# Feed-forward layers of a two-block network as one single chunk and five adjacent pairs, with another order of products inside a pair

## The chip, the cores and the metric

One Trainium2 chip, one of its cores. The metric is the device time of one execution in microseconds (us). Everything is computed in float32 inputs split into two parts (a "hi" part rounded to fp32r and a "lo" remainder), and one matrix product is made of three passes: hi x hi, lo x hi, hi x lo.

## The reference, cut to what matters

256 tokens of 1024 features run through two layers (a convolution module or an attention module, then a gated feed-forward network, then a small gate) and a second block. The change touches the two feed-forward networks alone:

```python
D_MODEL, SEQ, DEPTH = 1024, 256, 2
D_FF = 2816
def swiglu(x, w_gate, w_up, w_down):
    return (jax.nn.silu(x @ w_gate) * (x @ w_up)) @ w_down
...
u = rms_norm(h, ffn_norm_g[i])
h = h + swiglu(u, ffn_w_gate[i], ffn_w_up[i], ffn_w_down[i])
```

## The kernel before, in words

The 2816 hidden features of a layer are cut into 11 chunks (0 to 10) of 256; a chunk's 512 weight columns hold 256 of the gate and 256 of the up projection. The tokens are two tiles (t 0 and 1) of 128, the 1024 input features two halves.

**Weights.** A piece is 128x2048 float32 (1 MB). SP loads pieces into a ring of four (`raw`, line 385); the load of a piece waits until the lo part of the one four earlier is made. For each operand ScalarE (ACT) makes `w_hi` (line 1297) and then VectorE (DVE) `w_lo` (line 1857), both into rings of three: the hi part of operand g waits until TensorE (PE) is through with operand g-3. Both engines take the operands in stream order, at the places where the program calls `ahead(g)`, which feeds up to g+2. Each engine's instructions run in the order written, so an operand that is late holds up everything behind it.

**A single chunk** (`single`, `token_chunk`) is 48 matmuls of 512 columns: 2 halves x 2 tiles x 4 x 3 passes. A **pair** of chunks (`pair`, `product`) does the work of 96 in seven products of 12: B11, T1, T2, B22, B21, T4, T3. B11, B21 and B22 are pieces as loaded. T1 to T4 are sums of pieces, kept in three slots of `arena`: slot 0 for T1, slot 1 for T2 and then T3, slot 2 for T4. GpSimd (POOL) makes them with DMAs: a plain load and an accumulating one for T1 (lines 1164, 1106) and T4 (1168, 1109), one accumulating DMA on top of T2 for T3 (1156). DVE makes T2 out of T1 and the raw B22 (`second_sum`, line 1994). POOL issues them in this order for each next pair: T1's load (once T1's lo part is made), T3's addition (once T2's lo part is made), T1's addition, T4's load (once T4's lo part is made), T4's addition.

The products of a pair go to three of the PSUM banks 0 to 2 (b1, b4, b2), which rotate from pair to pair. Quarters are put together by ACT copies (`c_11` L1400, `c_22` L1404, `c_12` L1409) and DVE sums (L2046, L2049, L2038). `gated` (ACT silu L1361, DVE L1979) turns a quarter into the hidden values of one chunk and token tile. The last quarter, out of T3's bank, is gated by `last_quarter`, which runs on both engines at the start of the next step.

**Down projection.** `hidden_job(i)` (L603) transposes a chunk's hidden values, `hidden_hi` and `hidden_lo` (L1353, L1972) split them, `down(i)` is 24 matmuls of line 441 into banks 4 to 7. The steps of a layer are single 0, single 1, pairs (2,3), (4,5), (6,7), (8,9), single 10, and the order within a pair is

```python
product p1 B11; hidden_job(turned[0])
product p5 T1; product p6 T2; hidden_job(turned[1])
product p3 B22; down(within[0])
product p2 B21; product p7 T4; down(within[1])
product p4 T3
```

In the first feed-forward layer POOL issues, behind the last third sum, one further DMA that the attention needs much later (`toep`, line 1177).

## Time and profile before

| | |
|---|---|
| time, median of 3 runs | 1003.75 us (1002.15 to 1005.62) |
| the profiled execution's own time | 1003.63 us |
| its span | 1001.6 us |
| granted TensorE clock | 0.999 of full speed |
| busy: PE, DVE, ACT, POOL | 988.1, 775.3, 609.2, 153.6 us |
| first feed-forward layer (109.67 to 288.07 us) | 178.40 us |
| second feed-forward layer (429.39 to 605.35 us) | 175.96 us |

The span is the time from the first to the last instruction; about 2 us of the execution lie around it. A line of a timeline gives start, duration, engine, line, operation, tiles out<-in, shapes, and in brackets how long the engine had been idle and who ended that. Durations of neighbours overlap: one 512-column matmul is shown with 0.39 us though they start 0.227 us apart. So a product's length is read from start to start.

### The profile page before, as it was taken

To read this page: it belongs to the slowest core of one execution; us is meant where nothing else is said; L and a number is where in the kernel's file an instruction comes from. 1 tells how busy PE (TensorE), PEld (TensorE's weight loads), DVE (VectorE), ACT (ScalarE), POOL (GpSimd) and SP (SyncE) were. 2 spreads that over 40 slices of the span, in tenths; PEclk is the share of its full clock that TensorE was granted. 3 is DMA by queue.
4 is the path that set the end of the run, shared out by engine and by line. 5 is a ranking of instruction groups with operands and counts; after the bars stand their busy time and mean duration, and the time that the engine had idled before them with its cause. 6 is when DMAs were issued, how large, how long until landed. Compare 5 with 4: busy or idle time off the path is not lost.

```text
span 1001.6 us, 13597 instructions
## 1 busy us (share of the span) xinstructions
PE 988.1 (99%) x5350; PEld 835.5 (83%) x5350; DVE 775.3 (77%) x909; ACT 609.2 (61%) x722; POOL 153.6 (15%) x150
## 2 busy tenths in 40 slices
PE   8999999999999999999999999999999999999997
PEld 8977888888778888788888888788888889999886
DVE  6996888879567666787988857876877788777874
ACT  6437567657376668666676646754857574444733
POOL 4992101101030320111111002100100010000000
PEclk9999999999999999999999999999999999999999
DMA  8862899999784632779999864577789898545631
GB/s 324 256 217 90 274 298 324 334 300 305 209 292 161 238 128 85 256 264 300 331 343 338 256 218 167 189 256 280 262 258 341 237 311 299 186 169 179 220 126 43
DMA packets 37726, 242.01 MB, mean 242 GB/s; under 512 B 4504, under 2 KB 7064, under 8 KB 9760
## 3 DMA queue, kind: packets, MB, share of 16 engines
q1 hardware_dynamic: 23904, 167.26, 43.8%
q0 software_dynamic: 10736, 70.71, 28.2%
q10 hardware_dynamic: 3024, 3.18, 1.3%
q8 instruction: 43, 0.70, 0.3%
q14 instruction: 19, 0.16, 0.0%
HBM read 237.91 MB, written 3.21 MB: 241 GB/s over the span
## 4 chain that ended last, share of the span: by engine, by line
PE 80%; DVE 8%; DMA 6%; issue 3%; ACT 1%; POOL 0%; SPq 0%; ACTq 0%; POOLq 0%; DVEq 0%
PE bank L441 45%; PE bank L564 18%; DVE bank L2160 4%; PE bank L427 4%; PE bank L429 4%; PE bank L428 4%; DMA raw<-in_ws 4%; DMA arena<-in_ws 3%; PE bank L478 2%; DVE w_lo L1857 2%; PE bank L603 1%; PE bank L847 0%; DMA u_scr<-arena 0%; PE bank L944 0%; PE bank L977 0%
## 5 line engine op out<-in xcount | busy, mean ns | idle before, releaser
L1857 DVE TENSOR_TENSOR w_lo<-raw,w_hi 128x2048 fp32r<-128x2048 f32 x145 | 332.8, 2303 | 84.0 <-ACT w_hi L1297 83.7
L1297 ACT ACTIVATE w_hi<-raw 128x2048 fp32r<-128x2048 f32 x156 | 298.2, 1912 | 107.9 <-PE bank L441 71.3
L1297 ACT ACTIVATE w_hi<-arena 128x2048 fp32r<-128x2048 f32 x48 | 92.4, 1924 | 57.2 <-PE bank L441 21.0
L441 PE MATMUL bank<-w_hi,x_hi 128*128 128x512 f32 x416 | 115.0, 398 | 0.2
L1857 DVE TENSOR_TENSOR w_lo<-arena,w_hi 128x2048 fp32r<-128x2048 f32 x48 | 109.2, 2285 | 5.3 <-ACT w_hi L1297 5.2
L441 PE MATMUL bank<-w_lo,x_hi 128*128 128x512 f32 x416 | 111.5, 390 | 0.0
L441 PE MATMUL bank<-w_hi,x_lo 128*128 128x512 f32 x416 | 111.5, 390 | 0.0
L441 PE MATMUL bank<-w_hi,z_hi 128*128 128x512 f32 x320 | 94.2, 394 | 0.3 <-DVE z_lo L1972 0.3
L441 PE MATMUL bank<-w_lo,z_hi 128*128 128x512 f32 x320 | 92.9, 390 | 0.1
L441 PE MATMUL bank<-w_hi,z_lo 128*128 128x512 f32 x320 | 92.9, 390 | 0.0
L441 PEld LDWEIGHTS bank<-w_hi,x_lo 128*128 128x128 f32 x416 | 78.1, 188 | 16.8
L441 PEld LDWEIGHTS bank<-w_lo,x_hi 128*128 128x128 f32 x416 | 78.1, 188 | 16.5
L441 PEld LDWEIGHTS bank<-w_hi,x_hi 128*128 128x128 f32 x416 | 75.2, 188 | 16.3 <-issue 1.7
L428 PE MATMUL bank<-x_lo,w_hi 128*128 128x256 f32 x256 | 72.4, 283 | 0.0
L429 PE MATMUL bank<-x_hi,w_lo 128*128 128x256 f32 x256 | 72.4, 283 | 0.0
L427 PE MATMUL bank<-x_hi,w_hi 128*128 128x256 f32 x256 | 72.4, 283 | 0.0
L441 PEld LDWEIGHTS bank<-w_lo,z_hi 128*128 128x128 f32 x320 | 60.0, 188 | 13.1 <-DVE w_lo L1857 0.5
L441 PEld LDWEIGHTS bank<-w_hi,z_lo 128*128 128x128 f32 x320 | 60.1, 188 | 12.7
L441 PEld LDWEIGHTS bank<-w_hi,z_hi 128*128 128x128 f32 x320 | 58.8, 188 | 12.5 <-DVE z_lo L1972 0.7
L1069 POOL TENSOR_TENSOR w_lo<-raw,w_hi 128x2048 fp32r<-128x2048 f32 x11 | 50.7, 4615 | 110.9 <-ACT w_hi L1297 110.8
L564 PE MATMUL bank<-w_hi,q_hi 128*128 128x512 f32 x192 | 52.9, 397 | 1.0 <-ACT arena L1751 1.0
L564 PE MATMUL bank<-w_lo,q_hi 128*128 128x512 f32 x192 | 51.6, 391 | 0.0
(292 smaller groups left out, 1592.3 us busy)
## 6 DMA issues: line engine op xcount, KB each, us to landing
raw<-in_ws SPq DMA_DIRECT2D x156, 1024.0 KB, 7.3
arena<-in_ws POOLq DMA_DIRECT2D x60, 1024.0 KB, 11.4
arena<-u_scr ACTq DMA_DIRECT2D x16, 142.0 KB, 4.9
arena<-in_rows POOLq DMA_DIRECT2D x2, 1024.0 KB, 6.6
toep<-bias_row POOLq DMA_DIRECT2D x1, 1536.0 KB, 44.7
h<-in_x_tok SPq DMA_DIRECT2D x2, 512.0 KB, 4.0
raw<-in_ws SPq DMA_DIRECT2D x2, 512.0 KB, 8.0
arena<-in_rows POOLq DMA_DIRECT2D x2, 512.0 KB, 7.5
```

Of the source, the lines that this page charges most:

```text
L427: pe.matmul(dst, s_hi, m_hi, start=first, stop=False)
L428: pe.matmul(dst, s_hi, m_lo, start=False, stop=False)
L429: return pe.matmul(dst, s_lo, m_hi, start=False, stop=last)
L441: ins = pe.matmul(dst, tok(a_part, k, t), w_part[:, s, c], start=first and j == 0 and i == 0, stop=last and j == 2 and i == len(ks) - 1)
L478: ins = pe.transpose(banks[b][:, k * P:(k + 1) * P], src[:, k * P:(k + 1) * P], ident[:, :])
L564: ins = pe.matmul(banks[b][:, :], a_part[:, k, :], w_part[:, o % SPLIT, k * 512:(k + 1) * 512], start=start and j == 0 and k == 0, stop=j ...
L603: ins = pe.transpose(banks[t_bank][:, k * SEQ + t * P:k * SEQ + (t + 1) * P], hids[i % 3][:, t, k * P:(k + 1) * P], ident[:, :])
L1069: pool.tensor_tensor(w_lo[:, g % SPLIT, :], operand(g), w_hi[:, g % SPLIT, :].bitcast(F32), ALU.subtract).then_inc(S("lo_pool"), 1)
L1297: act.activation(w_hi[:, g % SPLIT, :], operand(g), ACT.Copy).then_inc(hi_done, 1)
L1857: dve.tensor_tensor(w_lo[:, g % SPLIT, :], operand(g), w_hi[:, g % SPLIT, :].bitcast(F32), ALU.subtract).then_inc(lo_done, 1)
L2160: ins = dve.scalar_tensor_tensor(out=y_odd[:, f % 2, :] if tap == TAPS - 2 else sums[c], in0=shifted, scalar=w, in1=sums[c], op0=ALU.mult, ...
```

## The change

Per layer: one single chunk (0) and five pairs (1,2) to (9,10) in place of three singles and four pairs. Within a pair B21 becomes the second product, and the two DVE steps that belong to it move with it. The first and the last pair hold one down product each, the others two, as before; three down products (7, 10, 9) stand behind the last pair. The banks are (b1, b4, b2) = (2, 1, 0) and (1, 2, 0) by turns. `second_sum` of the next pair is called after `ahead(T3)`, where it stood ahead of `ahead(o + 8)`.

```diff
-STEPS = (0, 1, (2, 3), (4, 5), (6, 7), (8, 9), 10)
+STEPS = (0, (1, 2), (3, 4), (5, 6), (7, 8), (9, 10))
-WITHIN = {(2, 3): (0, 1), (4, 5): (3, 2), (6, 7): (5, 4), (8, 9): (7, 6)}
-BEHIND = {10: (9, 8, 10)}
-TURNED = {(2, 3): (1, None), (4, 5): (3, 2), (6, 7): (5, 4), (8, 9): (7, 6), 1: (0,), 10: (9,)}
+WITHIN = {(1, 2): (0,), (3, 4): (2, 1), (5, 6): (4, 3), (7, 8): (6, 5), (9, 10): (8,)}
+BEHIND = (7, 10, 9)
+TURNED = {(1, 2): (0,), (3, 4): (2, 1), (5, 6): (4, 3), (7, 8): (6, 5), (9, 10): (8, 7)}
+FFN_ORDER = [("gu", 0, 0), ("gu", 0, 1)]
+for _p in PAIRS:
+    FFN_ORDER += [(_p, "B11"), (_p, "B21"), (_p, "T1"), (_p, "T2"), (_p, "B22"), ("down", WITHIN[_p][0]), (_p, "T4")]
+    FFN_ORDER += [("down", i) for i in WITHIN[_p][1:]] + [(_p, "T3")]
+FFN_ORDER += [("down", i) for i in BEHIND]
...
 TensorE, pair
-                    b1, b4, b2 = [(1 + PAIRS.index(p) + j) % 3 for j in range(3)]
+                    b1, b4, b2 = ((2, 1, 0), (1, 2, 0))[PAIRS.index(p) % 2]
                     product(("p1", n), ffn_at(layer, p, "B11"), *of_x(0, t0), b1, True, (S("c_11"), 2 * n - 1))
                     hidden_job(turned[0])
+                    product(("p2", n), ffn_at(layer, p, "B21"), *of_x(1, t0), b2, True, (S("c_11"), 2 * n))
                     product(("p5", n), ffn_at(layer, p, "T1"), *of_q(0), b4, True, (S("c_22"), 2 * n - 1))
                     product(("p6", n), ffn_at(layer, p, "T2"), *of_q(1), b1, False, (S("c_12"), 2 * n - 1))
-                    if turned[1] is not None:
-                        hidden_job(turned[1])
+                    for i in turned[1:]:
+                        hidden_job(i)
                     product(("p3", n), ffn_at(layer, p, "B22"), *of_q(2), b4, False, (S("c_12"), 2 * n))
                     down(within[0])
-                    product(("p2", n), ffn_at(layer, p, "B21"), *of_x(1, t0), b2, True, (S("c_11"), 2 * n))
                     product(("p7", n), ffn_at(layer, p, "T4"), *of_q(3), b1, False, (S("c_22"), 2 * n))
-                    down(within[1])
+                    for i in within[1:]:
+                        down(i)
...
+                for j, i in enumerate(BEHIND):
+                    if j + 1 < len(BEHIND):
+                        hidden_job(BEHIND[j + 1])
+                    down(i)
...
 ScalarE, pair
                     act.activation(c_11, bank[:, :], ACT.Copy).then_inc(S("c_11"), 1)
                     ahead(o + 1)
                     hidden_hi(turned[0])
+                    ahead(o + 2)
+                    act.wait_ge(S("c_11"), 2 * n)
+                    gated(one, 0, c_11[:, 0:256])
                     bank, _ = take(act, ("p5", n))
                     act.activation(c_22, bank[:, :], ACT.Copy).then_inc(S("c_22"), 1)
-                    ahead(o + 2)
+                    ahead(o + 3)
...
-                    ahead(o + 3)
                     ahead(o + 4)
+                    ahead(o + 5)
                     act.wait_ge(S("c_12"), 2 * n)
                     gated(two, 0, c_12[:, 0:256])
-                    ahead(o + 5)
                     ahead(o + 6)
-                    act.wait_ge(S("c_11"), 2 * n)
-                    gated(one, 0, c_11[:, 0:256])
                     act.wait_ge(S("c_22"), 2 * n)
                     gated(two, 1, c_22[:, 0:256])
-                    ahead(o + 7)
-                    ahead(o + 8)
+                    ahead(ffn_at(layer, p, "T3"))
...
 VectorE, pair
                     hidden_lo(turned[0])
                     ahead(o + 1)
+                    p_2, _ = take(dve, ("p2", n))
+                    dve.wait_ge(S("c_11"), 2 * n - 1)
+                    dve.tensor_tensor(c_11, p_2[:, :], c_11, ALU.add).then_inc(S("c_11"), 1)
                     ahead(o + 2)
+                    dve.wait_ge(S("c_11"), 2 * n)
+                    gated(one, 0, c_11[:, 256:512])
+                    for i in turned[1:]:
+                        hidden_lo(i)
+                    ahead(o + 3)
                     p_53, _ = take(dve, ("p3", n))
                     dve.wait_ge(S("c_12"), 2 * n - 1)
                     dve.tensor_tensor(c_12, p_53[:, :], c_12, ALU.subtract).then_inc(S("c_12"), 1)
-                    ahead(o + 3)
+                    ahead(o + 4)
                     dve.wait_ge(S("c_12"), 2 * n)
                     gated(two, 0, c_12[:, 256:512])
-                    ahead(o + 4)
                     ahead(o + 5)
                     u_3, _ = take(dve, ("p7", n))
                     dve.wait_ge(S("c_22"), 2 * n - 1)
                     dve.tensor_tensor(c_22, c_22, u_3[:, :], ALU.subtract).then_inc(S("c_22"), 1)
                     ahead(o + 6)
                     dve.wait_ge(S("c_22"), 2 * n)
                     gated(two, 1, c_22[:, 256:512])
-                    ahead(o + 7)
+                    ahead(ffn_at(layer, p, "T3"))
                     if p != PAIRS[-1]:
                         second_sum(PAIRS[PAIRS.index(p) + 1])
-                    ahead(o + 8)
```

On ScalarE and VectorE `first` (single 0) is the old `single(0)`, with `second_sum` of the first pair at its end on VectorE; `hidden_hi` and `hidden_lo` of `turned[1]` follow the new `ahead(o + 3)` on ScalarE and the gated step on VectorE.

## Rows read from the trace of the kernel before

**Rows 1.** The page, part 1: busy time, share of the span, instructions of each engine.
```profile
PE 988.1 (99%) x5350; PEld 835.5 (83%) x5350; DVE 775.3 (77%) x909; ACT 609.2 (61%) x722; POOL 153.6 (15%) x150
```

**Rows 2.** Busy time by stretch: both layers, one middle pair, and each layer's end.
```profile
core 0: us, PE busy (x) PEld busy (x) DVE busy (x) ACT busy (x) POOL busy (x), PEclk, DMA share, GB/s
429.39:605.35 175.96, 175.96 (x806) 145.60 (x805) 144.13 (x111) 113.80 (x105) 20.20 (x24) 1.00 0.89 290
109.67:288.07 178.40, 177.05 (x806) 145.16 (x804) 143.47 (x111) 111.57 (x103) 21.04 (x23) 1.00 0.93 295
...
482.94:513.86 30.92, 30.92 (x141) 25.56 (x140) 26.96 (x20) 21.32 (x18) 2.77 (x4) 1.00 1.02 317
...
256.50:288.70 32.20, 30.91 (x144) 24.84 (x144) 18.02 (x21) 15.09 (x21) 4.62 (x1) 1.00 0.75 247
...
575.70:605.35 29.65, 29.65 (x142) 24.49 (x141) 17.39 (x18) 14.60 (x19) 4.13 (x1) 1.00 0.57 208
```

**Rows 3.** Timeline, PE, second layer: a product, transposes, the next product, a down product.
```profile
441.17 1.07 PE L441 MATMUL bank<-w_hi,x_hi 128*128 128x512 f32 x4
...
485.67 0.60 PE L603 MATMUL bank<-ident,arena 128*128 128x128 f32 x4
486.03 1.18 PE L564 MATMUL bank<-w_hi,q_hi 128*128 128x512 f32 x4
...
488.88 1.07 PE L564 MATMUL bank<-w_hi,q_hi 128*128 128x512 f32 x4
...
494.82 0.61 PE L441 MATMUL bank<-w_hi,z_hi 128*128 128x512 f32 x2
...
500.26 1.07 PE L564 MATMUL bank<-w_hi,x_hi 128*128 128x512 f32 x4
```

**Rows 4.** Timeline, DVE, second layer: around the end of single 0.
```profile
443.22 2.29 DVE L1857 TENSOR_TENSOR w_lo<-raw,w_hi 128x2048 fp32r<-128x2048 f32 x1
445.43 0.48 DVE L1979 SCALAR_TENSOR_TENSOR arena<-bank,st,arena 128x256 f32<-128x256 f32 x1
445.82 2.28 DVE L1994 TENSOR_TENSOR arena<-arena,raw 128x2048 f32<-128x2048 f32 x1
```

**Rows 5.** Timeline, ACT, second layer: splits, a silu, a copy out of PSUM.
```profile
483.20 1.92 ACT L1297 ACTIVATE w_hi<-arena 128x2048 fp32r<-128x2048 f32 x1 [0.80 <-PE bank L564]
485.02 0.46 ACT L1361 ACTIVATE arena<-bank,st 128x256 f32<-128x256 f32 x1
...
492.25 0.60 ACT L1353 ACTIVATE z_hi<-bank 128x512 fp32r<-128x512 f32 x1 [0.76 <-PE bank L603]
492.74 0.59 ACT L1409 ACTIVATE arena<-bank 128x512 f32<-128x512 f32 x1
```

**Rows 6.** Timeline, DVE, second layer: two splits in a row, z_lo, a quarter's sum.
```profile
482.99 4.48 DVE L1857 TENSOR_TENSOR w_lo<-arena,w_hi 128x2048 fp32r<-128x2048 f32 x2
...
493.87 0.68 DVE L1972 TENSOR_TENSOR z_lo<-bank,z_hi 128x512 fp32r<-128x512 f32 x1
495.02 0.69 DVE L2038 TENSOR_TENSOR arena<-bank,arena 128x512 f32<-128x512 f32 x1 [0.47 <-PE bank L564]
```

**Rows 7.** Third sums of line 1156: four of the second layer, four of the first; then two alone.
```profile
DMA to landing us min/median/max: 9.5/13.9/16.4
...
DMA to landing us min/median/max: 8.4/14.9/19.0
...
DMA to landing us min/median/max: 13.8/13.8/13.8
...
DMA to landing us min/median/max: 16.3/16.3/16.3
```

**Rows 8.** Timeline, ACT, first layer: the hi part of T3 waits for its sum.
```profile
218.04 1.92 ACT L1297 ACTIVATE w_hi<-arena 128x2048 fp32r<-128x2048 f32 x1 [4.36 <-DMA arena<-in_ws]
```

**Rows 9.** The toep DMA of line 1177: issue to landing; PE's wait near the first layer's end.
```profile
DMA to landing us min/median/max: 44.7/44.7/44.7
...
275.07 0.65 PE L603 MATMUL bank<-ident,arena 128*128 128x128 f32 x4 [1.03 <-DVE z_lo L1972]
```

More of the change, by code:

```diff
@@ L1364, in ffn, with first @@
                 left = []
-                def single(i):
-                    g = ffn_at(layer, "gu", i, 0)
-                    ahead(g)
-                    while left:
-                        left.pop()()
-                    if i:
-                        hidden_hi(TURNED[i][0])
-                        ahead(g + 1)
-                    else:
-                        act.wait_ge(S("r_done"), m + 1)
+                def first():
+                    ahead(g0)
+                    act.wait_ge(S("r_done"), m + 1)
                     for t in range(TT):
-                        bank, _ = take(act, (("gu", layer, i), t))
-                        gated(i, t, bank[:, 0:256])
-                        if i == 0 and t == 0:
+                        bank, _ = take(act, (("gu", layer, 0), t))
+                        gated(0, t, bank[:, 0:256])
+                        if t == 0:
                             act.wait_ge(S("q_sums"), layer + 1)
@@ L1383, in single @@
                                            q_f32.rearrange("p i k c -> p (i k c)"), ACT.Copy).then_inc(S("q_hi"), 1)
-                            ahead(g + 1)
-                    behind = BEHIND.get(i, ())
-                    for j, k in enumerate(behind):
-                        if j + 1 < len(behind):
-                            hidden_hi(behind[j + 1])
-                        ahead(ffn_at(layer, "down", k))
+                            ahead(g0 + 1)
                 def pair(p):
@@ L1428, in pair @@
                     left.append(last_quarter)
-                for step in STEPS:
-                    if isinstance(step, tuple):
-                        pair(step)
-                    else:
-                        single(step)
+                first()
+                for p in PAIRS:
+                    pair(p)
+                left.pop()()
+                for j, i in enumerate(BEHIND):
+                    if j + 1 < len(BEHIND):
+                        hidden_hi(BEHIND[j + 1])
+                    ahead(ffn_at(layer, "down", i))
                 scaled_hi(m + 1, 0, 0, gname)
@@ L1994, in second_sum, with first @@
                     dve.tensor_tensor(sums[:, 1, :], sums[:, 0, :], raw[:, g % RAW, :], ALU.add).then_inc(S("t2"), 1)
[L1996 to L2010 removed]
+                def first():
+                    feed(g0 + 1)
+                    input_sums(m)
+                    ahead(g0)
                     for t in range(TT):
[L2012 to L2014 removed]
+                        bank, _ = take(dve, (("gu", layer, 0), t))
+                        gated(0, t, bank[:, 256:512])
+                        if t == 0:
                             input_lo(m)
[L2016 to L2021 removed]
+                            ahead(g0 + 1)
+                    second_sum(PAIRS[0])
                 def pair(p):
@@ L2049, in pair @@
                     dve.tensor_tensor(c_22, c_22, u_3[:, :], ALU.subtract).then_inc(S("c_22"), 1)
-                    dve.wait_ge(S("c_11"), 2 * n)
-                    gated(one, 0, c_11[:, 256:512])
                     ahead(o + 6)
@@ L2067, in ffn @@
                 dve.wait_ge(S("r_done"), m + 1)
-                for step in STEPS:
-                    if isinstance(step, tuple):
-                        pair(step)
-                    else:
-                        single(step)
+                first()
+                for p in PAIRS:
+                    pair(p)
+                left.pop()()
+                for j, i in enumerate(BEHIND):
+                    if j + 1 < len(BEHIND):
+                        hidden_lo(BEHIND[j + 1])
+                    ahead(ffn_at(layer, "down", i))
                 add_h(("ffn", layer, 0, 0), 0, 0)
```

73 lines of the change are left out of this document (12 added, 61 removed).

## The prediction

> **What bounds the kernel now.** The page's first part comes first: PE is busy 99% of the span [rows 1]. A busy PE can still stand in a stall between matmuls, so the second view is busy time by stretch. Both feed-forward layers run the same program; the second takes 175.96 us and the first 178.40 [rows 2]. Of the 2.44 us between them at least 1.29 are PE's idle time at the end (32.20 against 30.91 busy from 256.50 to 288.70); the second layer's end, 575.70 to 605.35, is full. A down product is 24 matmuls in 5.44 us (494.82 to 500.26), so one product of 12 is 2.72 us, and a hidden job costs 0.36 of its own and 0.13 in the product behind it [rows 3]. 744 matmuls x 0.2267 = 168.7, plus 11 hidden jobs (5.4) and the transposes of h, is the second layer's time: PE never waits there. The bound is PE, and the DMA engines are as full: share 1.02, 317 GB/s over one pair [rows 2]. That is 10 pieces (5 raw, 5 for sums, 10.49 MB) in 30.92 us, and third sums then take up to 16.4 and 19.0 us to land, against 9.5 and 8.4 us for the first ones [rows 7]; ACT has already waited 4.36 us for one [rows 8].
>
> **What goes.** Three singles and four pairs are 3 x 48 + 4 x 84 = 480 matmuls, one single and five pairs 48 + 420 = 468. The downs and the 11 hidden jobs stay. So PE sheds 12 matmuls, **2.72 us per layer**.
>
> **What is added beside PE.** Per layer 7 products replace 4 pieces: 3 hi and 3 lo splits, one second sum, five more DMAs for sums and one raw load less (4.2 MB on some 51). By 1.83 us an ACT split and 2.20 a DVE split in a row [rows 5, 6] that is 5.5 us of ACT and 8.8 of DVE in a layer where DVE is busy 144 of 176 us: room in the mean, so the order decides. I follow it step by step, with these steps: hi split 1.83 in a row, 1.92 to its end; lo split or second sum 2.20, 2.28 to its end; a 512-wide copy or z step 0.49 on ACT, 0.60 on DVE; a silu 0.42; a gated step 0.40, 0.48 to its end [rows 4 to 6]. From PE's end to ACT's start 0.26 us.
>
> **(a) Hidden job of chunk 0.** In the second layer B11 of pair (1,2) takes the place of single 1's first half, 441.17 to 443.89. Then PE wants to transpose chunk 0. Its second tile is gated by DVE at 445.43 to 445.91 [rows 4], behind q_lo and the lo part of piece 443.22; all of that DVE does in the same order as before. Before, 5.44 us of single 1 covered it; now 2.72 do. PE waits **2.1 us**, and B21, T1 and the rest are queued behind.
>
> **(b) B22 of pair (1,2).** T2's hi part waits for the second sum (445.82 + 2.28 = 448.10), then ACT runs z_hi, the hi part of B22, and then the silu of (one,0), which waits for DVE: T1's lo part, z_lo, T2's lo part (to 453.4), the sum c_11 (to 454.05). Only behind the silu comes the copy c_22, to 455.1, that frees B22's bank. PE is there at 454.4: **0.75 us**.
>
> **(c) A middle pair, sums in time.** Let S be the start of T1. PE: T1, T2, hidden job, B22, down, T4, down = 22.25 us. The hi part of the next B21 shares its slot with that down: 0.26 + 1.92. Then DVE, in order: lo of B21, second sum, lo of T1, each 2.20, and the last quarter, 0.48. T1 is the bank of the old T3, free only when that last quarter is gated. So S to S is 22.25 + 9.3 + 0.1 (the down product's lo part comes 9.65 after S and is wanted at 9.56) = 31.7 against 30.92: **0.8 us** for each of the turns 2-3, 3-4, 4-5. Before, this bank was the third one, and T1's start waited for nothing.
> By the order of the queues a third bank would give nothing back: T1 could start 0.7 us sooner, but the down product's lo part, 9.65 us behind the last quarter, would then be 0.8 us late.
> The Trainium skill (Perfetto Trace Analysis, Optimizing Tensor Performance, Matmuls) says that independent groups should rotate through different PSUM banks, so that one is emptied while the next runs. That speaks against two banks by turns; by it alone a third bank would be worth the 0.7 us of each turn, six of them, 4.2 us in all. No row of before shows a PE wait for a bank.
>
> **(d) The third sum.** T3's addition is issued when T2's lo part is done, now S + 3.1 where it was 4.8 us after B11's start before. Landed after L, the chain goes on: hi T3 1.92, lo T3 2.20, gated 0.40, lo B11, lo B21, second sum, lo T1 (8.8), gated 0.48 = 13.8. The turn is then **16.9 + L**, and L over 14.8 us stretches it. The rows of before have 13.8 and 16.4 (second layer), 16.3 and 19.0 (first) for such pairs [rows 7]: turns of 31.7, 33.3, 33.2, 35.9. A slower PE eases the DMA, so I take the middle between these and the floor of 31.7, with the third turn like the second. Second layer: floor 2.4, rows 5.6, taken 4.0. First: floor 2.4, rows 12.3, taken 7.4.
> In pair (1,2) no second down product stands between T4 and T3, and ACT takes T3's hi part ahead of the silu of (two,0), so the chain is 15.15 long and starts at 453.8 + L. With 9.5 us [rows 7] the next T1 starts at 478.4; by PE alone it would be at 474.9. **3.5 us** (2.4 with the first layer's 8.4; 0.8 is the floor).
> **The other queues.** POOL issues in the same order; the load for the next T1 now stands behind a lo part that is done at S - 0.4 and not 2.5 us after B11's start, 3 us later in the pair, and T1 is also wanted 3 us later. SP's raw loads wait for lo parts four pieces back, whose spacing stays; the second sum that holds B22's slot is still made ahead of B22's lo part. I put both at nothing; a late T1 sum would stretch a turn like (d) does.
>
> **(e) The end.** In pair (9,10) T3 follows T4 directly, and behind T3 PE wants chunk 10's hidden values, the second tile of which is gated behind T4's quarter and one more lo split: 0.8 us late at the least (the copies 0.2 + 0.6, lo 2.2, gated 0.48 against T3's 2.72). With the third sum late it is S + 3.1 + L + 8.15 against S + 19.5: 5.3 to 5.8 for an L of 13.5 to 14 (first layer's last one 13.5). Between 0.8 and 5.5 I take **3.1**.
>
> **(f) What goes besides.** The first layer's 2.44 us: the toep DMA (44.7 us [rows 9]) is now issued with four down products, T4, T3 and B22 ahead of PE and no single, so raw pieces are no longer wanted every 5.44 us from single and down both before it ends. Its first reader is in the attention, late enough either way. At nothing: the down products' new places, T1's and T4's sums (their two DMAs in series have a turn's length), the quarter sums; each lies under PE's next product, and costs its own 0.6 to 2.2 us if that cover goes.
>
> **Sum.** Second layer: -2.72 + 2.1 + 0.75 + 3.5 + 4.0 + 3.1 = +10.7. First: -2.72 + 2.1 + 0.75 + 2.4 + 7.4 + 3.1 - 2.44 = +10.6. On the profiled execution's own 1003.63 us (0.12 under the median shown): **1025.0 us**.
>
> **The rivals.**
> *Order waits only.* The DMA catches up, every third sum lands inside 14.8 us and no turn is longer than 31.7. For it: 13.8 and 9.5 in the rows; the slower PE gives 0.8 us a pair. Against: 10.49 MB at 317 GB/s is 33.1 us, more than 31.7. Second layer -2.72 + 2.1 + 0.75 + 0.8 + 2.4 + 0.8 = 4.1, first 1.7: **1009.4 us**.
> *DMA sets the pace throughout.* Landing times stay at those of before or grow. The upper ends: 14.7 + 17.9 = **1036 us**.
> *Faster.* One mechanism: the vector queue runs ahead of PE. In place of (c) and (d) the splits would have to be made early enough for T1 to find its bank free, which it does if the chain of 9.3 us from the down product's end were 8.6 or shorter, and the third sum of pair (1,2) landed in 6 us. Then (a) and (b) stay, 2.85 per layer, against 2.72, and the first layer's 2.44 go: 1003.63 + 0.26 - 2.44 = **1001.5**, or 1000.0 if (b) folds into (a). The ring of three w_hi slots, which starts the chain, speaks against it, and so does the shortest third sum of 8.4 us.
> *The change doesn't do what it says.* If some product were still issued twice, the count of 512-column matmuls would not fall by 24; the order list holds 7 per pair, so I give it no chance of its own.
>
> **How the numbers follow.** Forecast (1014 to 1031) 0.58, order waits only (1004 to 1014) 0.22, DMA pace (over 1031) 0.13, faster or even 0.07. The range 1007 to 1035 leaves out 2 in 10 at most. 0.3%, about what a measurement of this kernel can tell, is 3 us: of the last case 0.04 is faster and 0.03 the same, and 0.01 of the order waits lies within 3 us. So faster 0.04, same 0.04, slower 0.92.
>
> **What would show it.** PE waits about 2 us at its first hidden job (L603) in both layers, on DVE L1979; B22 of pair (1,2) waits on ACT's c_22 copy; T1 of each later pair waits on DVE L1979; S to S is 31.7 or more, and 16.9 plus the third sum's landing time where that is over 14.8; the wait near 275 us is gone. Wrong would be: no PE wait at the first hidden job, or turns of 30.9 us, which would mean that I have the queue order wrong.

## The result and the profile after

| | before | after |
|---|---|---|
| time, median of 6 runs each | 1004.38 us (1002.15 to 1005.69) | 1040.95 us (the profiled one 1043.07) |
| ratio | | 1.0354, 95% interval 1.0321 to 1.0387 |
| span, granted clock | 1001.6 us, 0.999 | 1041.2 us, 0.987 |
| first, second feed-forward layer | 178.40, 175.96 us | 198.01, 193.94 us |

36.6 us slower; 21.3 had been forecast. One of the six runs, 1084.93 us, was in a slower state of the chip: the ratio leaves it out, and without it the median is 1039.67. The direction was right and the size was not. First the page's busy times (as [rows 1]) and busy time by stretch (as [rows 2], with its columns, here and below): the two layers, one middle pair, a product T3, and the first matmuls behind the first layer.

```profile
PE 997.6 (96%) x5326; PEld 835.8 (80%) x5326; DVE 796.2 (76%) x923; ACT 621.1 (60%) x734; POOL 160.8 (15%) x160
```
```profile
109.94:307.95 198.01, 179.24 (x794) 144.09 (x792) 153.64 (x118) 118.23 (x110) 23.00 (x28) 0.97 0.94 285
450.98:644.92 193.94, 181.52 (x793) 145.34 (x792) 154.36 (x118) 119.68 (x111) 23.51 (x29) 0.97 0.92 285
537.02:569.17 32.15, 31.47 (x141) 25.41 (x141) 26.99 (x20) 21.16 (x19) 3.47 (x6) 1.00 1.01 318
493.40:498.66 5.26, 5.25 (x12) 4.11 (x13) 5.26 (x4) 2.20 (x2) 0.00 (x0) 0.50 0.87 333
307.95:311.50 3.55, 3.55 (x9) 2.78 (x10) 3.55 (x7) 2.72 (x5) 2.29 (x1) 0.50 0.47 155
```

PE is no longer full: it is idle for 19 us in the first layer and 12 in the second. And in two of the stretches the granted clock is 0.50 (1.2 of 2.4 GHz): a product of 12 matmuls takes 5.26 us where it took 2.72 [rows 3]. The timeline of PE, second layer, shows where:

```profile
467.56 0.44 PE L599 MATMUL bank<-ident,arena 128*128 128x128 f32 x2 [1.69 <-DVE arena L1956]
...
476.90 1.17 PE L560 MATMUL bank<-w_hi,q_hi 128*128 128x512 f32 x4 [0.51 <-ACT arena L1382]
...
493.40 2.05 PE L560 MATMUL bank<-w_hi,x_hi 128*128 128x512 f32 x4 [4.89 <-DVE arena L2014]
495.25 1.91 PE L560 MATMUL bank<-w_hi,x_lo 128*128 128x512 f32 x4
...
569.17 1.15 PE L560 MATMUL bank<-w_hi,q_hi 128*128 128x512 f32 x4 [0.65 <-DVE arena L1956]
...
604.00 1.17 PE L560 MATMUL bank<-w_hi,q_hi 128*128 128x512 f32 x4 [2.56 <-DVE arena L1956]
605.01 1.86 PE L560 MATMUL bank<-w_hi,q_lo 128*128 128x512 f32 x4
...
623.88 1.17 PE L560 MATMUL bank<-w_hi,x_hi 128*128 128x512 f32 x4 [0.87 <-DVE arena L2014]
...
626.73 0.60 PE L599 MATMUL bank<-ident,arena 128*128 128x128 f32 x4
```

In order: the hidden job of chunk 0; B22 of pair (1,2); T3 of pair (1,2), 5 us late and at half clock; T1 of two later pairs; T3 of the last pair and the hidden job behind it, which doesn't wait. ACT and then DVE around that T3:

```profile
487.56 1.91 ACT L1284 ACTIVATE w_hi<-arena 128x2048 fp32r<-128x2048 f32 x1 [6.70 <-DMA arena<-in_ws]
489.38 0.49 ACT L1348 ACTIVATE arena<-arena,st 128x256 f32<-128x256 f32 x1
```
```profile
489.97 0.48 DVE L1956 SCALAR_TENSOR_TENSOR arena<-arena,st 128x256 f32<-128x256 f32 x1 [6.29 <-ACT arena L1348]
490.38 2.28 DVE L1834 TENSOR_TENSOR w_lo<-arena,w_hi 128x2048 fp32r<-128x2048 f32 x1
492.58 0.68 DVE L2014 TENSOR_TENSOR arena<-arena,bank 128x512 f32<-128x512 f32 x1
```

ACT waits for the third sum, makes T3's hi part, and only then the silu of (two,0). Behind that silu DVE gates, makes T3's lo part, and only then subtracts T4's quarter (L2014), which frees the bank into which T3 goes. So T3 starts 4 us after its hi part is there. (T4 itself ends near 488.5, so a subtraction right behind it would still leave a wait of 0.9 us.) Landing of the third sums (as [rows 7]; second layer, first layer) and of the toep DMA (as [rows 9]), and what ACT saw of that last one:

```profile
DMA to landing us min/median/max: 10.8/12.1/17.8
...
DMA to landing us min/median/max: 9.8/12.2/13.7
...
DMA to landing us min/median/max: 40.7/40.7/40.7
```
```profile
303.68 1.91 ACT L1284 ACTIVATE w_hi<-raw 128x2048 fp32r<-128x2048 f32 x1 [13.08 <-DMA raw<-in_ws]
```

The time by place, from T1's starts in the two profiled executions. "PE alone" is the sum of PE's work at full clock: 11.78 to B11 [rows 2, 3], products of 2.72, down products of 5.44, hidden jobs and the two last transposes of h of 0.49; a full turn, from one T1's start to the next, is 30.92.

| place | PE alone | first, second layer | over, first / second | forecast, first / second |
|---|---|---|---|---|
| layer's start to the first T1 | 17.71 | 19.60, 19.60 | 1.9 / 1.9 | 2.1 / 2.1 |
| first to second T1 (pair (1,2)) | 24.97 | 34.21, 34.31 | 9.2 / 9.3 | 3.2 / 4.3 |
| three middle turns | 92.76 | 96.37, 99.11 | 3.6 / 6.4 | 7.4 / 4.0 |
| last T1 to the next stage | 37.80 | 47.83, 40.92 | 10.0 / 3.1 | 3.1 / 3.1 |
| layer | 173.24 | 198.01, 193.94 | 24.8 / 20.7 | 15.8 / 13.4 |

Less 2.72 for the 12 matmuls, and less 2.44 of before in the first, this is +19.6 and +18.0, and 1.7 more lie in the next stage, which starts at half clock: 39.3 of the 39.4 us between the two profiled executions. Two places make up the miss: pair (1,2), and the first layer's end with the start of the stage behind it.

### The profile page after: what moved, and what is told of

It is laid out like the page before. It is cut to its first block, busy times and chain, and to the rows that moved or that the text cites. A ratio compares the mean times of both kernels' runs of the same rounds, so it can differ in the third digit from the quotient of the medians.

```text
span 1041.2 us, 13611 instructions
## 1 busy us (share of the span) xinstructions
PE 997.6 (96%) x5326; PEld 835.8 (80%) x5326; DVE 796.2 (76%) x923; ACT 621.1 (60%) x734; POOL 160.8 (15%) x160
## 4 chain that ended last, share of the span: by engine, by line
PE 66%; DVE 12%; DMA 10%; issue 7%; ACT 4%; POOL 1%; POOLq 0%; ACTq 0%; DVEq 0%
PE bank L437 37%; PE bank L560 13%; DMA arena<-in_ws 8%; DVE w_lo L1834 5%; DVE bank L2125 4%; PE bank L423 4%; PE bank L425 4%; PE bank L424 4%; DMA raw<-in_ws 2%; PE bank L474 2%; ACT w_hi L1284 2%; DVE arena L1971 1%; PE bank L673 1%; PE bank L834 0%; ACT z_hi L1340 0%
## 5 line engine op out<-in xcount | busy, mean ns | idle before, releaser
L1284 ACT ACTIVATE w_hi<-arena 128x2048 fp32r<-128x2048 f32 x56 | 107.7, 1924 | 98.2 <-DMA arena<-in_ws 51.4
L1834 DVE TENSOR_TENSOR w_lo<-arena,w_hi 128x2048 fp32r<-128x2048 f32 x56 | 128.0, 2286 | 11.4 <-ACT w_hi L1284 11.2
L437 PE MATMUL bank<-w_hi,x_hi 128*128 128x512 f32 x352 | 98.5, 402 | 8.1 <-issue 7.9
L437 PE MATMUL bank<-w_hi,x_lo 128*128 128x512 f32 x352 | 95.2, 392 | 0.0
L437 PE MATMUL bank<-w_lo,x_hi 128*128 128x512 f32 x352 | 94.4, 390 | 0.0
L437 PEld LDWEIGHTS bank<-w_hi,x_hi 128*128 128x128 f32 x352 | 64.0, 190 | 22.3 <-issue 10.0
L437 PEld LDWEIGHTS bank<-w_hi,x_lo 128*128 128x128 f32 x352 | 66.7, 189 | 14.5
L437 PEld LDWEIGHTS bank<-w_lo,x_hi 128*128 128x128 f32 x352 | 66.2, 188 | 14.1
L560 PE MATMUL bank<-w_hi,q_hi 128*128 128x512 f32 x224 | 61.6, 397 | 7.9 <-DVE arena L1956 5.8
L437 PEld LDWEIGHTS bank<-w_hi,z_hi 128*128 128x128 f32 x320 | 58.9, 188 | 12.1 <-issue 0.5
L560 PE MATMUL bank<-w_lo,q_hi 128*128 128x512 f32 x224 | 61.1, 395 | 0.0
## 6 DMA issues: line engine op xcount, KB each, us to landing
arena<-in_ws POOLq DMA_DIRECT2D x70, 1024.0 KB, 11.5
```

The lines of the kernel that those rows point to most:

```text
L437: ins = pe.matmul(dst, tok(a_part, k, t), w_part[:, s, c], start=first and j == 0 and i == 0, stop=last and j == 2 and i == len(ks) - 1)
L560: ins = pe.matmul(banks[b][:, :], a_part[:, k, :], w_part[:, o % SPLIT, k * 512:(k + 1) * 512], start=start and j == 0 and k == 0, stop=j ...
L1284: act.activation(w_hi[:, g % SPLIT, :], operand(g), ACT.Copy).then_inc(hi_done, 1)
L1834: dve.tensor_tensor(w_lo[:, g % SPLIT, :], operand(g), w_hi[:, g % SPLIT, :].bitcast(F32), ALU.subtract).then_inc(lo_done, 1)
```

## The experiments

All times are medians; "changed kernel" is 1040.95. Each run had the kernel before measured beside it (medians 1002.75 to 1004.99), and a ratio is against that. The runs on the clock, T3's bank, the second bank, the old order, chunk 0 and the second toep version have ratios of 1.0325 to 1.0354, all inside the changed kernel's interval of 1.0321 to 1.0387. Their totals alone don't tell them from it; what they show is read from their profiles. Only the line that carries each edit is shown.

**The clock.** 20 matmuls that nobody reads, in front of T3 of pair (1,2).

```diff
+                    if p == PAIRS[0]:
+                        begin(t_bank)
+                        for _ in range(20):
+                            pe.matmul(banks[t_bank][:, :], x_hi[:, 0, 0:P], x_hi[:, 0:2, :]..., start=True, stop=True)
                     product(("p4", n), ffn_at(layer, p, "T3"), ...)
```


> The changed kernel, but ahead of T3 of pair (1,2) TensorE runs 20 matmuls of 512 columns into the transposes' bank, whose result nobody reads (4.5 us at full clock), where it now idles for 5 us. Nothing else moves. Theory 'the idle time halves the clock of what comes behind it': T3 starts as before (493.4), but lasts 2.7 and not 5.26 us at a granted clock of 1.0; the next T1 comes 2.1 us sooner (then VectorE's chain is next), so 4 us in all for both layers, 1036 to 1038. Rival 'T3 is slow because of its operand or the bank, not of the clock': T3 still takes 5.2 us and the time stays within 1.5 us.

1038.68 us. PE's timeline and the clock of the same stretch:

```profile
486.68 4.70 PE L649 MATMUL bank<-x_hi 128*128 128x512 f32 x20
491.21 1.07 PE L560 MATMUL bank<-w_hi,x_hi 128*128 128x512 f32 x4
492.12 1.07 PE L560 MATMUL bank<-w_hi,x_lo 128*128 128x512 f32 x4
```
```profile
484.00:500.00 16.00, 16.00 (x74) 13.03 (x72) 13.03 (x10) 11.63 (x10) 1.14 (x2) 1.00 0.98 304
```

T3 takes 2.72 us again, the clock stays at 1.00, and the next T1 comes 2.2 and 3.3 us sooner than in the changed kernel. So the idle 5 us, not the operand, cost the other 2.5. The Trainium skill (TensorE: Matmul & The Clock Gate, HAM oscillation — how this bites in real kernels) describes this: a wait for a DMA lets the clock fall, and the work behind it starts cold. These traces agree, with a wait for VectorE in place of one for a DMA.

Not all of the 2.2 and 3.3 us is the clock's. From POOL's issue of the third sum to the next T1, second layer, changed kernel and then this one:

```profile
475.43 0.85 POOL L1143 DMA_DIRECT2D arena<-in_ws  x1 [2.68 <-DVE w_lo L1834]
...
504.89 1.07 PE L560 MATMUL bank<-w_hi,q_hi 128*128 128x512 f32 x4
```
```profile
473.77 0.85 POOL L1148 DMA_DIRECT2D arena<-in_ws  x1 [2.67 <-DVE w_lo L1839]
...
484.49 1.92 ACT L1289 ACTIVATE w_hi<-arena 128x2048 fp32r<-128x2048 f32 x1 [5.29 <-DMA arena<-in_ws]
...
499.93 1.16 PE L560 MATMUL bank<-w_hi,q_hi 128*128 128x512 f32 x4
```

The sum took 12.1 us there and 10.7 here (12.2 and 11.8 in the first layer). Less that, 17.3 us are left in the changed kernel and 15.4 here (17.1 and 15.4 in the first): the half clock cost the next T1 1.9 and 1.7 us, and with the clock full what is left is within 0.3 us of the forecast's chain of 15.15, although T3 still starts 3.9 and 4.8 us after its hi part is there. The late bank cost the next T1 its time through the clock.

**T3's bank.** In the pairs with one down product the silu of (two,0), on DVE also T4's quarter sum, now stand ahead of T3's operand (`ahead(o + 5)`).

```diff
-                    ahead(o + 5)
+                    if len(WITHIN[p]) == 2:
+                        ahead(o + 5)
```


> The changed kernel, but in the two pairs that hold one down product, (1,2) and (9,10), ScalarE's silu of (two,0) and VectorE's quarter sum c_22 come ahead of T3's hi and lo part, so that T3's bank is free before T3's operand is made. Theory 'T3 of pair (1,2) waits for its bank behind its own operand': T3 then starts when its hi part ends, near 489.5 in place of 493.40 in the second layer and 148.5 in place of 152.46 in the first, the wait of 5 us falls to about 1 to 1.5 us, the half clock behind it goes (2.5 us), and the next T1 comes 2.5 to 3.6 us sooner (its chain of four lo parts and a second sum on VectorE is next): 5 to 7 us for both layers, plus 1 to 2 for the two last pairs; 1032 to 1035. Rival 'the late third sum alone counts' (12.2 us to land): T3's wait only changes its name to the operand, and the time falls by under 2 us.

1038.12 us. T3 of pair (1,2), second layer:

```profile
490.99 1.17 PE L560 MATMUL bank<-w_hi,x_hi 128*128 128x512 f32 x4 [0.87 <-DVE arena L2016]
```

The wait is 0.87 and T3's clock full; first to second T1 is 30.6 us in both layers, 3.6 and 3.7 less, of which 0.4 and 1.7 are third sums that landed sooner (11.8 and 10.4 us). But the first layer's middle turns went from 32.1 to 33.95, 33.4 and 33.0: a faster PE met later sums (17.0, 16.4 and 16.05 us), and 4 of the 7 us were given back. The total missed its 1032 to 1035. These turns are 16.9 + L once more, to 0.1 us. The half clock came back one step later, in the first layer behind the wait of the next T1:

```profile
159.75 1.15 PE L560 MATMUL bank<-w_hi,q_hi 128*128 128x512 f32 x4 [2.54 <-DVE arena L1957]
160.74 1.84 PE L560 MATMUL bank<-w_hi,q_lo 128*128 128x512 f32 x4
```

**The second bank.** `last_quarter`, which frees T3's bank for the next T1, ahead of T1's lo part on DVE.

```diff
-                    ahead(o)
+                    feed(o + 1)
                     while left:
                         left.pop()()
+                    ahead(o)
```


> The changed kernel, but VectorE gates the last quarter (which frees T3's bank for the next T1) ahead of T1's lo part and not behind it; nothing else moves. It frees that bank 2.2 us sooner, more than a third bank would be worth. The prediction said that this gives nothing back, because the down product's lo part would then be late by as much: turn stays at 32.1 us, time within 1 us of the changed kernel. Rival, a mechanism of the order: VectorE is seen idle for 0.8 to 1.3 us ahead of the second hidden chunk's z_lo, waiting for TensorE's own transposes, so all behind it comes sooner as well when TensorE does: turn 31.3 us, T1's wait of 0.8 us goes in all eight turns, 5 to 6.5 us in all.

T1 no longer waits, and then the down product does. PE in the last middle turn:

```profile
573.49 0.73 PE L437 MATMUL bank<-w_lo,z_hi 128*128 128x512 f32 x2 [1.16 <-DVE w_lo L1834]
```

Turns went from 32.13 to 31.95, 0.2 us less, near the forecast's (c), which had said nothing at all. The total, 1035.45 us (ratio 1.0286 to 1.0379), is lower, but its interval overlaps that of the changed kernel, and its profile has the gain where nothing was moved (third sums that landed sooner in pair (1,2)). How far the edit itself helps stays open.

**The second sum.** Ahead of the next B21's lo part, in DVE's idle 2 us.

```diff
-                    ahead(ffn_at(layer, p, "T3"))
+                    feed(ffn_at(layer, p, "T3") + 1)
                     if p != PAIRS[-1]:
                         second_sum(PAIRS[PAIRS.index(p) + 1])
+                    ahead(ffn_at(layer, p, "T3"))
```


> The changed kernel, but VectorE makes the next pair's second sum ahead of the next B21's lo part and no longer behind it, where it now idles for 1.96 us (527.8 to 529.8) until ScalarE has that piece's hi part. Theory 'the turn of 32.1 us is VectorE's queue behind the second down product': the second sum fills the idle time, T1's bank is free 2.0 us sooner and the down product's lo part too, so no wait is left and the middle turns fall to 31.0 us: 1.1 us in each of six turns, 6 to 7 us, 1034 to 1036. Rival 'the sum for T1 itself lands no sooner' (it was issued 17 us before and took 14.5 us): VectorE then waits at the second sum for the DMA, and the turn stays at 32 us or gets longer.

1051.56 us (ratio 1.0445 to 1.0509), slower than the changed kernel beyond the noise. Turns of 32.0 and 32.2 stayed and others grew to 34.0, 35.5 and 37.0, with third sums of up to 19.6 us in the first layer and 17.3 in the second. Turns got longer, as the rival said, but DVE's wait at the second sum, the rival's reason, is only 0.4 and 1.1 us in the two longest. Why the sums came so late was not followed further.

**Third sum and order, two by two.** The third sum adds 64 columns in place of 2048 (T3's product is as long, on a sum that lacks the rest), with the new order and with the old one on one single and five pairs.

```diff
-                pool.dma_start(sums[:, 1, :], ws[...], accum_op=ALU.add)
+                pool.dma_start(sums[:, 1, 0:64], ws[...][:, 0:64], accum_op=ALU.add)
```
```diff
-    FFN_ORDER += [(_p, "B11"), (_p, "B21"), (_p, "T1"), (_p, "T2"), (_p, "B22"), ("down", WITHIN[_p][0]), (_p, "T4")]
+    FFN_ORDER += [(_p, "B11"), (_p, "T1"), (_p, "T2"), (_p, "B22"), ("down", WITHIN[_p][0]), (_p, "B21"), (_p, "T4")]
...
-                    b1, b4, b2 = ((2, 1, 0), (1, 2, 0))[PAIRS.index(p) % 2]
+                    b1, b4, b2 = [(2 + PAIRS.index(p) + j) % 3 for j in range(3)]
```


> The changed kernel, but the third sum adds 64 of the 2048 columns, so that it lands at once and 10% of the layer's DMA traffic is gone (T3's product is computed on a wrong operand of the same size). Theory 'the late third sum counts in the first and the last pair, and the middle turns are set by the order of the queues': the middle turns stay at 32.1 us; T3 of pair (1,2) waits 0.9 us and not 5, at full clock, and the next T1 comes about 6 us sooner in each layer; the turn of 34.8 goes to 32.1; 1022 to 1027 in all. Rival (the forecast's d) 'the third sum stretches the middle turns too': turns below 31.8 us and a time below 1018.

> One single chunk and five pairs as in the changed kernel, but inside a pair the order of the kernel before: B21 behind the first down product, its two VectorE steps, the second sum's place and the three rotating banks as before. Theory 'the order inside the pair costs the middle turns and the third sum's late issue': the middle turns are 30.9 to 31.4 us (32.1), the third sum is issued about 3 us earlier in the pair and T3 of pair (1,2) waits 2 to 3 us; 1014 to 1024, with the toep wait of about 8 to 10 us still there. Rival 'the number of pairs costs, whatever the order' (10% more DMA traffic per layer): turns of 32 us and more, 1035 or above.

> One single chunk and five pairs, the order inside the pair of the kernel before, and the third sum of 64 columns, so that it lands at once and 10% of the layer's DMA traffic is gone. With the full third sum the middle turns were 30.92 once and 32 to 34.4 otherwise. Theory 'those longer turns are the DMA's, and the new order has a floor of its own of 32.1 us': here all middle turns are 30.92 us, the second layer takes 178 to 181 us (183.6 with the new order and the small third sum), 1009 to 1015 in all. Rival 'the old order has its own waits on VectorE with five pairs too': turns of 31.5 or more, and a time within 3 us of the new order's 1023.3.

| | third sum whole | 64 columns |
|---|---|---|
| new order | 1040.95; turns 32.1, one 34.8 | 1023.32; all 32.1 |
| old order | 1035.52; turns 30.9, 33.1, 32.2 / 31.0, 33.8, 32.5 | 1018.33; all 30.9 |

Middle pairs, new order (T1 to T1) and then old (T4 to T4), both with the small sum:

```profile
521.28:553.36 32.08, 31.41 (x140) 25.41 (x141) 26.88 (x20) 21.18 (x19) 3.73 (x6) 1.00 0.98 302
```
```profile
534.64:565.51 30.87, 30.87 (x141) 25.56 (x140) 26.96 (x20) 21.31 (x18) 3.64 (x5) 1.00 1.00 311
```

By the medians the third sums cost 17 us in either order and the order 5 us with either sum. By the ratios it is 15 and 18, and 3 and 6: with the small sum the order's part is clear of the noise, with the whole one it is not (1.0321 to 1.0387 against 1.0302 to 1.0348). The new order has a floor of 32.1 us a turn that is its own. The old one has none, yet with whole sums five pairs in a row don't hold 30.9, as four did [rows 2]: my expectation of 1014 to 1024 for it missed, and with the small sum I was right on the turns and 3 us too low on the whole. With the small sum the second layer of the new order takes 183.59 us, 10.4 over PE alone with nothing late; the other 10.35 of its 193.94 are late sums and the clock behind them.

**Late by shared traffic, or by kind?** The third sum whole, T4's addition 64 columns (`sums[:, 2, 0:64]`; the rest of that sum is left out).

> The changed kernel, with the third sum whole but T4's addition of 64 of the 2048 columns: the same 10% of DMA traffic gone, from another sum. Theory 'third sums are late because all sums and pieces share the DMA engines': they land in 8 to 10 us instead of 10 to 18, T3 of pair (1,2) waits 1.5 to 3 us instead of 4.9, the middle turns stay at 32.1 and none is longer; 1027 to 1034. Rival 'a third sum takes 12 us of its own, being an accumulating DMA behind GpSimd's others': T3's wait stays at 4 to 5 us and the time within 3 us of the changed kernel.

1029.99 us. Third sums, second layer:

```profile
DMA to landing us min/median/max: 8.4/8.5/8.7
```

The same DMA of 1 MB, 8.5 us in place of 12.1 and up to 17.8, because another one is gone. T3 of pair (1,2) waits 1.55 (4.89), the middle turns are 32.1 and none is longer. So a third sum is late by what other DMAs move, not by its own kind. The DMA that is gone stood on GpSimd's queue too: whether its share of the 16 engines or its place in that queue mattered, this run does not separate.

**Start of the layer.** Chunk 0 transposed behind B21 of pair (1,2).

```diff
                     product(("p2", n), ffn_at(layer, p, "B21"), ...)
                     if p == PAIRS[0]:
+                        hidden_job(turned[0])
```


> The changed kernel, but TensorE transposes chunk 0 behind B21 of pair (1,2) and not ahead of it, so that B21 covers the 1.7 us in which it waited for chunk 0's second tile. Nothing else moves. Theory 'the forecast's (a) and (b) are one chain on VectorE' (q_lo, B21's lo part, second sum, T1's lo part, z_lo, T2's lo part, B22's): the wait at the hidden job goes, but T1's lo part is still done near 471.8 and the copy c_22 near 476.8, so TensorE waits there instead, B22 starts within 0.3 us of 476.9 - (467.56) = 9.3 us behind the old time of the hidden job, and the time stays within 1.5 us of the changed kernel. Rival 'two separate waits' (as the forecast added them): 2.0 us per layer, 4 in all, 1037.

1038.54 us. PE, first layer (from 109.94 in both kernels):

```profile
130.94 1.20 PE L560 MATMUL bank<-w_lo,q_hi 128*128 128x512 f32 x4 [1.30 <-DVE w_lo L1836]
...
135.88 1.17 PE L560 MATMUL bank<-w_hi,q_hi 128*128 128x512 f32 x4 [0.52 <-ACT arena L1384]
```

B22 starts at 135.88; in the changed kernel it was 135.87. The wait of 1.7 us is gone, one of 1.30 for DVE stands inside T1, and B22 is no sooner; the ratio is 1.0354 as before. (a) and (b) are one chain on DVE.

**The toep DMA.** Moved behind the layer (after `h_factor(1)`); the same with `h_factor(2)` ahead of the wait for its landing; and, in the kernel before, up to the convolution stage near 56 us and, last, behind the layer with its read-back behind the first step of the attention.

```diff
             h_factor(1)
+            pool.dma_start(toep, bias_row[:, :]...)
+            h_factor(2)
             pool.wait_ge(S("toep_out"), 16)
```


> The changed kernel, but the first feed-forward layer's toep DMA is issued after h_factor(1), when that layer is over, and no longer behind its last third sum. In the changed kernel it took 40.7 us to land, ScalarE waited 13.08 us for a raw piece from 290 on, and the first matmul behind the layer came 7.95 us late and then ran at half clock (2.7 us). Theory 'toep starves the raw loads': the wait and the half clock go, the layer from 109.94 ends at about 299.8 instead of 307.95, and the time falls by 8 to 11 us, to 1030 to 1033. Rival 'the raw loads are late anyway, from the sums of the last pairs': under 2 us, and the wait stays. A third outcome, the DMA collides with the next stage's loads instead: the wait at 303 goes and one of 3 us or more appears between 310 and 345.

> The changed kernel, but the toep DMA is issued after h_factor(1) and h_factor(2) stands ahead of the wait for its landing. With the DMA there alone (the run before, 1044.8 us), the 13 us wait for a raw piece was gone, but GpSimd stood behind the landing at 344.8 and gave h_factor(2) 14 us late: TensorE waited 11.27 us. Theory: both waits go, 8 to 11 us less than the changed kernel, 1030 to 1033. Rival: the readers of toep in the attention (370 us) or GpSimd's steps at 354 now wait for the read-back; then a wait of more than 2 us stands there, and the gain is under 6 us.

> The kernel before with the same one edit: the toep DMA near 62 us in the convolution stage. It lost 2.44 us at the end of its first layer against the second. Theory: that goes, 1001 to 1002, 0.2 to 0.3% faster. Rival: the DMA disturbs the start of the first layer, whose pieces are asked for from 80 us on; 1004 or more.

> The kernel before, with the toep DMA issued after h_factor(1), when its first feed-forward layer is over, and its read-back behind h_factor(2) and GpSimd's first step of the attention (the changed kernel with the read-back one place earlier still had waits of 1.42 and 2.78 us there; 9 us are enough for the read-back before its reader near 350). Theory 'the 2.44 us of the first layer against the second are the toep DMA's': that goes and nothing comes in its place, 2 to 3 us, 1000 to 1001, ratio 0.997 to 0.998. Rival 'the DMA costs the same wherever it stands': within 1 us of before.

Both versions of the changed kernel had been expected at 1030 to 1033. With the DMA behind the layer the starved piece is gone and the first layer takes 191.87 and 190.49 us (198.01). The first version, 1044.84 us, loses it again: PE, then GpSimd, behind which `h_factor(2)` stood.

```profile
348.82 2.05 PE L437 MATMUL bank<-w_hi,x_hi 128*128 128x512 f32 x4 [11.27 <-ACT arena L1582]
```
```profile
344.83 0.93 POOL L1168 DMA_DIRECT2D arena<-toep  x1 [35.17 <-DMA toep<-bias_row]
```

The second, 1038.35 us, keeps part of it: waits of 1.42 and 2.78 us stand in the attention. In the kernel before, the convolution stage paid (1025.86 us):

```profile
93.02 6.47 PE L754 MATMUL bank<-arena 128*32 128x256 f32 x64 [11.50 <-issue]
```
```profile
65.00:80.00 15.00, 6.39 (x69) 2.93 (x62) 10.39 (x27) 0.92 (x2) 10.39 (x6) 0.72 0.56 95
80.00:95.00 15.00, 3.50 (x24) 1.83 (x26) 0.00 (x0) 0.03 (x1) 0.00 (x0) 0.61 0.46 78
```

Its matmuls are fed by small DMAs that ACT issues. Here is how long these took, from 56 to 95 us, in the kernel before and in this run:

```profile
arena<-u_scr ACTq DMA_DIRECT2D x4, 142.0 KB, 4.8
```
```profile
arena<-u_scr ACTq DMA_DIRECT2D x4, 142.0 KB, 18.3
```

They were late while GpSimd's DMA ran, at 78 to 95 GB/s in all. The Trainium skill (DMA: Bandwidth & Descriptors, Issuing engines are not separate DMA queues) says that another issuing engine is no other DMA hardware; the trace agrees. Its first layer then took 175.96 us, exactly the second's: the 2.44 us were the toep DMA's. In the changed kernel the same early place gave 1054.44 (1030 to 1033 expected). The last version, 1004.04 us (ratio 0.9999 to 1.0021), has the first layer at 176.53 (-1.9) and the attention at 143.63 (141.32, +2.3): in the kernel before, this DMA costs 2 us at the layer's end and as much behind it, and 22 in the convolution stage.

**The edits together, and what is left.** Toep moved as in that last version, T3's bank and last quarter as above; then with the first down product's lo part ahead of the second z_lo on DVE; then that with the small third sum.

```diff
-                    for i in turned[1:]:
-                        hidden_lo(i)
                     ahead(o + 3)
+                    for i in turned[1:]:
+                        hidden_lo(i)
```


> The changed kernel with the toep DMA and its read-back placed in that way, the quarter sum c_22 ahead of T3's operand in the pairs with one down product, and the last quarter ahead of T1's lo part. The same two edits with the toep DMA's fault in the attention gave 1040.8 us, of which 13 to 14 lay in the attention (11.69 us and a half clock). Theory: 1025 to 1030; what is left over before is the order's own waits and the third sums, so no rearrangement of these queues reaches 1004. Rival: the DMA traffic gives back half of the 13 us; 1033 or more.

> The kernel with all three edits (1025.35 us), and VectorE makes the first down product's lo part ahead of z_lo of the second hidden chunk and not behind it. That z_lo waits 0.8 us for ScalarE's z_hi, and the down product was seen to wait 0.7 to 1.3 us for the lo part behind it. Theory 'the floor of 32.0 us is only the order of VectorE's queue': the wait goes, the middle turns are 30.9 to 31.2 us (31.9 to 32.0 before this edit where no sum was late), about 5 us in all, 1019 to 1022. Rival 'at 31 us a turn the DMA engines are the bound' (10.49 MB in 31 us are 338 GB/s): sums land later, turns of 32 us and more stay, 1024 or above.

> The same kernel with a third sum of 64 columns, so 10% less DMA traffic. If the order's floor is gone, all six middle turns are 30.9 to 31.2 us here whatever the DMA did in the run before, and the time is 1009 to 1014: what is left over the kernel before is the start and the end of the layers (2.8 us at the start, about 2 each in pair (1,2), its next T1 and the last pair, less 2.72). If turns stay at 32 us, the floor has another cause than the two lo parts moved so far.

1025.35, 1027.78 and 1016.38 us. (T3's bank, the last quarter and the toep DMA simply behind the layer gave 1040.83, where 1016 to 1021 had been expected; 11.7 us of it were the same wait in the attention.) Two middle pairs with the whole sum, two with the small one:

```profile
523.24:556.17 32.93, 31.97 (x141) 25.20 (x140) 26.21 (x20) 19.97 (x19) 4.24 (x6) 1.00 1.02 327
556.17:588.37 32.20, 31.93 (x140) 25.43 (x141) 27.11 (x20) 20.93 (x19) 3.06 (x5) 1.00 1.01 314
```
```profile
517.87:548.79 30.92, 30.92 (x141) 25.56 (x140) 26.89 (x20) 21.05 (x20) 3.64 (x5) 1.00 0.98 305
548.79:579.71 30.92, 30.92 (x141) 25.57 (x140) 27.01 (x20) 21.16 (x20) 3.65 (x5) 1.00 0.99 309
```

With both lo parts moved the order's floor is gone: 30.92 to the hundredth, in two turns of three. With whole sums the turns stay at 32.2 to 35.3, and ACT waits for the sum:

```profile
544.39 1.92 ACT L1285 ACTIVATE w_hi<-arena 128x2048 fp32r<-128x2048 f32 x1 [7.28 <-DMA arena<-in_ws]
```

So the queue order had a floor at 32.1, and with it gone the whole third sums still hold the turns at 32.2 and more. That this second floor is the rate of the DMA engines is argued, not shown: 10.49 MB in 32.1 us are 327 GB/s, the engines are as busy (1.00 to 1.02), but in the kernel before the same ten pieces a turn went through at 30.92 in three turns in a row. The first two edits and the toep DMA win back 16 of 37 us by the medians, 11 by the ratio (1.0244 against 1.0354); the moved down product's lo part adds nothing clear of the noise with whole sums (1.0225). With three edits and the small sum (1016.38) my 1009 to 1014 still was too low, by the first turn behind pair (1,2), 32.2 and not 30.9. No version beat the kernel before.

## Why the prediction was wrong

- **What goes** (2.72 per layer): right; PE alone is 173.24.
- **(a), (b)**: right in size. PE lost 1.9 by the hidden job at L599 and 0.9 at B22, 2.8 in all for 2.85. They are one chain, and adding them was right only because (b) had been counted from the delayed PE.
- **(c)** floor of 31.7 for a middle turn: mechanism right, size off: 32.13. A third bank gives nothing: with that bank free 2.2 us sooner a turn shrank by 0.2. The Trainium skill's rule on rotating PSUM banks (Perfetto Trace Analysis, Optimizing Tensor Performance, Matmuls), 4.2 us in all by it alone, does not decide here: the bank was not the only thing late. But "nothing" held only with DVE's order as it was; with the next lo part moved too, and the small third sum, 30.92 was reached.
- **(d), pair (1,2)**: the step that failed. With (b) in it, 3.2 / 4.3 was forecast and 9.2 / 9.3 measured. The larger part is the size of L: I took the landing times of the first third sums before, 8.4 and 9.5, and these sums took 12.2 and 12.1, 3.8 and 2.6 us more at the next T1. The chain behind the landing was right: 15.15 forecast, 15.4 with the clock full. What no term had is the clock. I let T3's product start when its hi part is ready; it also needs the bank of T4's quarter, whose subtraction stands on DVE behind T3's own lo part and behind a silu that waits for T3's hi part. PE waited 4.9 us, 4.0 of them behind a finished hi part, and then ran T3 at half clock, which cost the next T1 1.7 and 1.9 us. That T1 of pair (3,4) waits for nothing, against the sign given, is this too: PE was later than DVE.
- **(d), middle turns**: 16.9 + L with L over 14.8 was right as a rule: with 9.8 to 13.7 every turn of the first layer was 32.1. It was mis-sized there (7.4 for 3.6), since a slower PE eased the sums more than I took. The stretched turn of the second layer (34.8, L = 17.8: 16.9 + L is 34.7) fits the rule, and so do the longer turns of the run on T3's bank.
- **The other queues**, at nothing: right, save what the toep DMA did.
- **(e)**: 3.1 forecast, 3.1 in the second layer, by luck. The wait that I had priced, for chunk 10's hidden values behind T3, is not there (626.73). In its place 1.7 us are half clock behind the 2.56 us that the last T1 waited, and 1.0 is T3's wait for its bank; in the first layer the same stretch lost 2.0. Where T3's bank was freed first, the hidden job does wait, 1.18 us.
- **(f)**: the wrong sign. I let the toep DMA become harmless and took 2.44 us off. It starved a raw piece for 13.08 us; the next stage started 8 us late at half clock, 8.0 in the layer and 1.7 behind it. I had looked at which pieces the layer itself still wanted, not at the first piece of the next stage.
- **The clock** was in no term. In [rows 2] it is 1.00 throughout, in a kernel where PE's longest idle time in these layers is 1.03 us; the forecast itself brought waits of 2.1 to 3.5 us and did not ask what they would do to it.
- The rival "DMA sets the pace throughout" (1036) was nearest in size, and late third sums are what the five pairs ran into once the order's waits were taken away.

## What to carry to other kernels

Where a matmul accumulates into a bank, list what must happen before it twice: for the operand and for the bank; and look whether one of the two stands behind the other on a queue. When a forecast puts a wait of several microseconds on a TensorE that never idled, add what the work behind it costs at half clock. In these runs, with the DMA engines at a share of 1.0, a faster order met later landings (T3's bank freed first: 4 of 7 us given back); so price a change first by the bytes that it needs in a turn.

## What was not expected of the hardware

- An idle time of 4.9 us on PE and then 5.26 us for 12 matmuls of 512 columns (0.50 of full clock). Behind 2.56 us (changed kernel) and 2.54 (T3's bank, first layer) two groups of four took near 1.9 us each; behind 2.58 (T3's bank, second layer), 2.54 (the clock run) and 2.51 (chunk 0) none did. What decides between them, these runs do not show.
- One DMA of 1.5 MB out of 8 partitions took 35 to 47 us, and DMAs of two other engines waited meanwhile, 13 us for a piece of 1 MB and 11.5 us for small ones, while the total was 78 to 95 GB/s in the convolution stage.
- A third sum of 64 columns still took 2.3 to 13.5 us to land: its own bytes, 32 KB, do not set its landing time; most likely the DMAs queued before it do, which no run separates.
